# A ring of eight expert units instead of six, expert sums added straight into the residual, and a gather with the third tile's parts stacked on 128 rows

## What is computed

```python
def moe(x, router_w, router_b, w1, b1, w2, b2):
    logits = (x @ router_w).astype(jnp.float32) + router_b
    top_v, top_i = lax.top_k(logits, TOP_K)          # 4 of 32 experts
    gates = jax.nn.softmax(top_v, axis=-1)
    ...
    def expert_block(args):
        xblk, e = args
        hdn = xblk @ w1[e] + b1[e]                   # 1024 -> 2 x 1024
        g, up = hdn[:, :D_FF], hdn[:, D_FF:]
        g = jnp.minimum(g, SWIGLU_LIMIT)
        up = jnp.clip(up, -SWIGLU_LIMIT, SWIGLU_LIMIT)
        act = (up + 1.0) * (g * jax.nn.sigmoid(g * SWIGLU_ALPHA))
        return act @ w2[e] + b2[e]                   # 1024 -> 1024
...
    h2 = rmsnorm(x, ln_ffn_g) * (1.0 + sc2) + sh2
    f = moe(h2.reshape(B * L, D), ...)
    x = x + g2 * f
```

## Time and profile before

| | us |
|---|---|
| median of 3 runs | 1584.41 (1583.7 to 1587.89) |
| profiled execution | 1582.1 |
| its span, first to last instruction | 1580.3 |
| PE busy | 1483.1 (94%) |
| DVE busy | 527.3 (33%) |
| ACT busy | 336.7 (21%) |
| DMA, mean over the span | 313 GB/s, 495.14 MB |
| dense part and router | 0 to 594 |
| expert loop, 34 blocks | 594 to 1561 |
| mean granted TensorE clock | 0.974 of full |

### The profile page before, as it was taken

How to read it: one execution, slowest core, us unless ns; L and a number is a source line. 1 busy time by engine, 2 the same in 40 slices (tenths; PEclk the granted TensorE clock), 3 DMA queues, 4 the chain that set the end, 5 groups by cost and what they waited for, 6 DMA issues and landing times.

```text
span 1580.3 us, 20912 instructions
## 1 busy us (share of the span) xinstructions
PE 1483.1 (94%) x8280; PEld 626.6 (40%) x8281; DVE 527.3 (33%) x899; ACT 336.7 (21%) x607; POOL 131.2 (8%) x119
## 2 busy tenths in 40 slices
PE   4989899999999969999999999999999999999995
PEld 3456455554555443333333333333333333333331
DVE  2132124545257352332323323323333232332225
ACT  2123332212223232121211211211212121121110
POOL 0000001113238503000000000000000000000000
PEclk9989999999999969999999999999999999999997
DMA  9653533242324948999999999998877999999993
GB/s 345 236 233 134 237 135 132 89 143 88 120 94 148 315 176 336 429 429 428 429 428 428 429 428 429 428 429 365 335 302 290 430 427 430 427 429 428 428 430 136
DMA packets 40264, 495.14 MB, mean 313 GB/s; under 512 B 5316, under 2 KB 5860, under 8 KB 11428
## 3 DMA queue, kind: packets, MB, share of 16 engines
q1 hardware_dynamic: 35700, 480.18, 73.4%
q0 software_dynamic: 4528, 14.46, 3.3%
HBM read 490.14 MB, written 4.47 MB: 313 GB/s over the span
## 4 chain that ended last, share of the span: by engine, by line
PE 66%; DMA 27%; DVE 3%; ACT 2%; issue 1%; POOL 1%; SPq 0%; DVEq 0%
DMA ring<-in_w_moe 24%; PE ps L1759 20%; PE ps L1382 17%; PE ps L1785 9%; PE ps L1393 4%; PE ps L1713 3%; PE ps L1698 3%; PE ps L1335 3%; DMA ring<-in_w_dense 1%; PE ps L1351 1%; DMA T<-mod_rows 1%; DMA consts<-in_consts 1%; PE ps L1447 1%; PE ps L1766 1%; PE ps L1474 1%
## 5 line engine op out<-in xcount | busy, mean ns | idle before, releaser
L1759 PE MATMUL ps<-ring,arena 128*64 128x512 f32 x2176 | 485.5, 596 | 17.0 <-DMA ring<-in_w_moe 16.8
L1382 PE MATMUL ps<-ring,xT 128*128 128x512 f32 x672 | 302.7, 607 | 5.8 <-DMA ring<-in_w_dense 5.7
L1759 PEld LDWEIGHTS ps<-ring,arena 128*64 128x64 f32 x2176 | 150.9, 137 | 313.2 <-issue 271.0
L1785 PE MATMUL ps<-ring,arena 128*64 128x512 f32 x1088 | 248.5, 598 | 0.0
L1306 DVE SCALAR_TENSOR_TENSOR U<-ps,arena,U 128x1024 f32<-128x1024 f32 (+1 forms) x102 | 130.5, 1280 | 180.5 <-PE ps L1713 180.5
L1382 PEld LDWEIGHTS ps<-ring,xT 128*128 128x128 f32 x672 | 127.3, 193 | 159.8 <-issue 152.5
L1785 PEld LDWEIGHTS ps<-ring,arena 128*64 128x64 f32 x1088 | 72.1, 136 | 145.4 <-issue 130.9
L1297 DVE TENSOR_SCALAR arena<-ps 128x512 f32<-128x512 f32 x34 | 23.5, 692 | 241.5 <-PE ps L1766 241.5
L816 ACT ACTIVATE xT<-ps 128x512 f32<-128x512 f32 x35 | 20.9, 598 | 332.9 <-PE ps L1698 318.9
L1713 PE MATMUL ps<-xT,arena 64*128 64x512 bf16 x630 | 87.2, 384 | 2.9 <-DVE xT L1312 2.9
L1393 PE MATMUL ps<-ring,xT 128*64 128x256 f32 x672 | 78.6, 388 | 0.0
(11 more groups left out here) (298 smaller groups left out, 1166.6 us busy)
## 6 DMA issues: line engine op xcount, KB each, us to landing
ring<-in_w_moe SPq DMA_DIRECT2D x192, 2048.0 KB, 20.2
ring<-in_w_dense SPq DMA_DIRECT2D x33, 2048.0 KB, 8.5
V<-in_state POOLq DMA_DIRECT2D x6, 256.0 KB, 7.2
out_sample_retention<-V POOLq DMA_DIRECT2D x6, 256.0 KB, 4.9
arena<-in_b POOLq DMA_DIRECT2D x9, 128.0 KB, 2.8
R<-in_x_prompt SPq DMA_DIRECT2D x1, 1024.0 KB, 10.6
arena<-in_cache_kT POOLq DMA_DIRECT2D x8, 128.0 KB, 3.6
arena<-in_cache_v POOLq DMA_DIRECT2D x8, 128.0 KB, 4.0
```

The source lines that it names most:

```text
L1382: last = mm(banks[t][0], xT[:, k, t * P:t * P + P], wv[:, k, :], start=(k == 0), stop=(k == KD - 1))
L1759: last = mm(ps[64 * a:64 * a + 64, half, :], xgT[:, k, j % 2, :], wv[:, k, HALF * a:HALF * a + HALF], start=(j % 2 == 0 and k == 0), stop= ...
L1785: last = mm(ps[64 * a:64 * a + 64, 2, :], actT[:, k, j - 4, :], wv[:, k, HALF * a:HALF * a + HALF], start=False, stop=(j == 5 and k == 3), ...
```

## The change

**Ring.** `SLOTS` goes from 6 to 8: a unit may be loaded as soon as the one eight before it is used. The two new slots lie where `V`, `U` and `T` were: `memory` is one buffer of 8 x 4096 + 1024 columns, slot 6 covers V and the first row of U, slot 7 the other rows of U and two rows of T. Units 0 and 1 of expert 1 are loaded into them before the loop, the first after `x1_ready`, the second after `h_split`. Since 24 units (four experts) fill eight slots three times, the loops of SP and PE are written out for four experts: PE's block body stands four times, in a loop over groups of four, each with an inner loop over the blocks of its expert.

**Sums.** `U` is no longer an accumulator. Each scatter is multiplied by gate and gate2 rows into `grown` and added to R at once. The gate2 rows lie in dead parts of `mod` and in T's last row block; DVE waits for them (`gate2_in`) before its loop, no longer behind it.

**Gather.** ACT writes the middle part of tile 2 a second time to rows 64 to 127 beside its high part (`packed`), and doubles the tile's slot numbers (`slots_doubled`); one matmul on 128 rows then takes both.

```diff
-SLOTS = 6
+SLOTS = 8
+SPARE_SLOTS = 3
...
-    ring = sb("ring", [P, SLOTS, 4096])
+    memory = sb("memory", [P, SLOTS * 4096 + D])
+    ring = memory[:, 0:SLOTS * 4096].rearrange("p (s c) -> p s c", s=SLOTS)
+
+    def in_late_slots(n):
+        at = (DENSE_SLOTS + SPARE_SLOTS) * 4096 + 3 * D * n
+        return memory[:, at:at + 3 * D].rearrange("p (t d) -> p t d", t=3)
+
+    V, U, T = in_late_slots(0), in_late_slots(1), in_late_slots(2)
...
-    h_low = [V[:, 1, 0:HALF], V[:, 1, HALF:D], after_router[:, 1792:1792 + HALF]]
+    gate2 = [after_mod[:, 0:D], after_mod[:, 0:D], T[:, 2, :]]
+    h_low = [after_mod[:, D:D + HALF], low_1[:, :], W[:, 2, HALF:D]]
     h_parts = [[W[:, t, 0:HALF].bitcast(BF16), W[:, t, HALF:D].bitcast(BF16), h_low[t].bitcast(BF16)] for t in range(3)]
+    packed = W[:, 2, 0:HALF].bitcast(BF16)
...
@@ SP
         load_expert_unit(2)
+        load_rows(gate2[0], 10, gate2_in)
+
+        def load_second_expert(j):
+
+            sp.dma_start(ring[:, EXPERT_UNITS + j, :], ins["w_moe"][1, j, :, :]).then_inc(unit_in[EXPERT_UNITS + j], 16)
+
         sp.wait_ge(x1_ready, 3)
-        load_rows(V[:, 0, :], 10, gate2_in)
-        load_rows(V[0:64, 2, :], 10, gate2_in)
+        load_second_expert(0)
+        sp.wait_ge(h_split, 3)
+        load_second_expert(1)
+        load_rows(gate2[2][0:64], 10, gate2_in)
         sp.wait_ge(table_ready, 1)
...
+        with sp.Fori(0, NEXP // 4 - 1) as g:
+            for u in range(4 * EXPERT_UNITS):
+                if u % EXPERT_UNITS == 0:
+                    blocks = blocks_before(4 * g + (u // EXPERT_UNITS + 1))
+                e, j = divmod(u + SLOTS, EXPERT_UNITS)
+                sp.wait_ge(unit_used, EXPERT_UNITS * blocks + u % EXPERT_UNITS)
+                sp.dma_start(ring[:, u % SLOTS, :], ins["w_moe"][bass.ds(4 * g + e, 1), j, :, :].rearrange("a p n -> p (a n)")).then_inc(unit_in[u % SLOTS], 16)
...
@@ POOL
-        nc.gpsimd.memset(U[:, :, :], 0.0).then_inc(sum_clean, 1)
@@ ACT
+            if t == 2:
+                A(packed[64:128], T[0:64, t, :], ACT.Copy).then_inc(mid_moved, 1)
...
+        act.wait_ge(slots_placed, 1)
+        A(slot_of[64:128, 2, :], slot_of[0:64, 2, :], ACT.Copy).then_inc(slots_doubled, 1)
@@ DVE
-        dve.wait_ge(sum_clean, 1)
+        dve.wait_ge(slots_doubled, 1)
         dve.wait_ge(table_ready, 1)
         n_blocks = dve.value_load(table_i[0:1, MAX_BLOCKS:MAX_BLOCKS + 1], min_val=NEXP, max_val=MAX_BLOCKS - 1)
+        dve.wait_ge(gate2_in, 16 * (1 + BATCH_S))
...
             for t, r in enumerate(ROWS):
                 dve.wait_ge(scattered, 3 * i + t - 2)
-                both = U[0:r, t, :].rearrange("p (a b) -> p a b", a=2)
-                X.scalar_tensor_tensor(out=both, in0=ps[0:r, 6:8, :], scalar=gate_last[0:r, t:t + 1], in1=both, op0=ALU.mult, op1=ALU.add).then_inc(added, 1)
-            dve.wait_ge(added, 3 * i + 1)
+                X.scalar_tensor_tensor(out=halves(grown[0:r]), in0=ps[0:r, 6:8, :], scalar=gate_last[0:r, t:t + 1], in1=halves(gate2[t][0:r]),
+                                       op0=ALU.mult, op1=ALU.mult).then_inc(added, 1)
+                dve.wait_ge(added, 3 * i + t - 1)
+                X.tensor_tensor(R[0:r, t, :], R[0:r, t, :], grown[0:r], ALU.add).then_inc(summed, 1)
+                dve.wait_ge(summed, 3 * i + t - 2)
...
-        dve.wait_ge(gate2_in, 16 * (1 + BATCH_S))
-        for t, r in enumerate(ROWS):
-            X.tensor_tensor(U[0:r, t, :], U[0:r, t, :], V[0:r, 2 if t == 2 else 0, :], ALU.mult).then_inc(scaled, 1)
-            dve.wait_ge(scaled, t + 1)
-            X.tensor_tensor(R[0:r, t, :], R[0:r, t, :], U[0:r, t, :], ALU.add).then_inc(summed, 1)
-            dve.wait_ge(summed, t + 1)
...
@@ PE
             for t, r in enumerate(ROWS):
-                for m, part in enumerate(h_parts[t]):
+                parts = [(part, r) for part in h_parts[t]] if t < 2 else [(packed, P), (h_parts[t][2], r)]
+                for m, (part, rows) in enumerate(parts):
...
-        with pe.Fori(1, n_blocks + 1) as i:
-            e = pe.value_load(table_i[0:1, bass.ds(i - 1, 1)], min_val=0, max_val=NEXP - 1)
+
+        def expert_block(i, g, c):
+
+            def unit(j):
+                u = EXPERT_UNITS * c + j
+                pe.wait_ge(unit_in[u % SLOTS], 48 * g + 16 * (filled(u % SLOTS) + u // SLOTS + 1))
+                return ring[:, u % SLOTS, :].rearrange("p (k c) -> p k c", k=4)
...
+        with pe.Fori(0, NEXP // 4) as g:
+            for c in range(4):
+                before = pe.value_load(table_i[0:1, bass.ds(4 * g + (MAX_BLOCKS + 1 + c), 1)], min_val=0, max_val=MAX_BLOCKS - 1)
+                through = pe.value_load(table_i[0:1, bass.ds(4 * g + (MAX_BLOCKS + 2 + c), 1)], min_val=1, max_val=MAX_BLOCKS - 1)
+                with pe.Fori(before + 1, through + 1) as i:
+                    expert_block(i, g, c)
```

More of the change, by code:

```diff
@@ L1245, in _ @@
             aux_taken(dve, name)
-            done(X.tensor_scalar(s, s, 1.0, None, ALU.subtract))
+            done(X.tensor_scalar(s, s, 1.0, None, ALU.subtract), slots_placed if t == 2 else dve_step)
         done(X.tensor_copy(sel_now[:, 0, :], slot_of[:, :, 0]))
@@ L1323, in _ @@
             first = FINAL_BANKS[t]
[L1324 to L1327 removed]
+            X.scalar_tensor_tensor(out=halves(grown[0:r]), in0=ps[0:r, first:first + 2, :], scalar=gate_last[0:r, t:t + 1], in1=halves(gate2[t][0:r]),
+                                   op0=ALU.mult, op1=ALU.mult).then_inc(grown_last, 1)
+            dve.wait_ge(grown_last, t + 1)
+            X.tensor_tensor(R[0:r, t, :], R[0:r, t, :], grown[0:r], ALU.add).then_inc(final_ready, 1)
+            dve.wait_ge(final_ready, t + 1)
     @block.tensor
@@ L1695, in gather @@
             for t, r in enumerate(ROWS):
-                for m, part in enumerate(h_parts[t]):
+                parts = [(part, r) for part in h_parts[t]] if t < 2 else [(packed, P), (h_parts[t][2], r)]
+                for m, (part, rows) in enumerate(parts):
                     for a in range(2):
-                        last = mm(ps[64 * a:64 * a + 64, 3, :], pick[0:r, t, 0, :], part[0:r, HALF * a:HALF * a + HALF],
-                                  start=(t == 0 and m == 0), stop=(t == 2 and m == 2), skip_group_check=True)
+                        last = mm(ps[64 * a:64 * a + 64, 3, :], pick[0:rows, t, 0, :], part[0:rows, HALF * a:HALF * a + HALF],
+                                  start=(t == 0 and m == 0), stop=(t == 2 and m == 1), skip_group_check=True)
             last.then_inc(gathered, 1)
@@ L1754, in _ @@
                 for j in (2 * half, 2 * half + 1):
-                    pe.wait_ge(unit_in[j], 16 * e + 16 * (filled(j) + 1))
-                    wv = ring[:, j, :].rearrange("p (k c) -> p k c", k=4)
+                    wv = unit(j)
                     for k in range(4):
@@ L1773, in _ @@
             pe.wait_ge(act_ready, i)
-            for c in range(4):
-                last = tr(ps[:, 4, c * P:(c + 1) * P], h_act[:, c * P:(c + 1) * P], P)
+            for k in range(4):
+                last = tr(ps[:, 4, k * P:(k + 1) * P], h_act[:, k * P:(k + 1) * P], P)
             last.then_inc(actT_done, 1)
```

49 lines of the change are left out of this document (27 added, 22 removed).

## The result

The changed kernel takes 1573.43 us (median, 1569.57 to 1576.89) where the kernel before, on the same chip, takes 1587.72 (1583.7 to 1592.17): ratio 0.9906, 95% interval 0.9885 to 0.9927, faster by 14.3 us. The forecast, 1567.3 from 1584.4, is a ratio of 0.9892 and a gain of 17.1. The profiled execution took 1569.57 us, its span is 1567.8; against 1580.3 before that is 12.5 us less.

A forecast was written before the change was run, and what follows sets the result against it. PE and DMA were both taken as near their limit in the expert loop. Gains of 10.7 (block 18 to 34), 0.2 (block 34's gather) and 6.2 (tail) sum to 17.1 us: 1584.4 to 1567.3 us, range 1563.5 to 1577.5.

The forecast's parts named there:

- What bounds the kernel, and the sum of stages: PE and DMA both near their limit in the expert loop; gains 10.7 + 0.2 + 6.2 = 17.1 us.
- The ring in the gaps: Two DMA gaps at experts with two blocks: two more slots give 9.79 us of lead, once, not twice.
- Rival (b): The weight stream restarts no further on, the ring doing nothing: gain 7.3 us, 1577.1 us; chance 0.05.
- The start of the stream: Before the loop: unit 7's lead 1.7 us, net shift of the weight stream 0, from -1.7 to +4.3 us.
- Rival (c): The weight stream starts up to 4.3 us late for the row copies, all passed to block 18: 1571.6; chance 0.05.
- DVE's wait: DVE's first loop copy, now behind gate2_in, moves 7 us later, leaving PE 6.3 us late; price nothing.
- The gather: Third tile, 6 matmuls become 4: saves 0.215 us per block, 3.4 us from block 18 to block 34.
- Rival (a): The gather saves nothing, the change of row count eating it: gain 13.6 us, 1570.8 us; chance 0.09.
- Sums and tail: DVE's extra adds in the loop all hidden; the tail after the last block 6.2 us shorter.
- PE's loop at cost 0: PE's extra table read per expert and outer branch per four stay hidden, its sequencer being 2.4 us ahead: cost 0.
- (d): PE's fourfold loop needs one small code transfer at each return, 1.6 us beyond what is hidden: 1572.1; chance 0.08.
- (e): PE's code pages come one after another behind the weight stream, 10.8 us not hidden per return: slower, 1630; chance 0.05.

The follow-up runs named there:

- ring of six: The changed kernel with six slots instead of eight, the old loop start and nothing loaded ahead for the second expert: 1581.53 us, ratio 0.9972.
- late stream: The changed kernel with its last eight row copies made three times, each set waited for, ahead of unit 7: 1578.57 us, ratio 0.996.
- rows first: The changed kernel with the last eight row copies of gate2 ahead of unit 7 instead of behind it: 1570.55 us, ratio 0.9916.

## Why the prediction was right, step by step

- **What bounds the kernel, and the sum of stages.** Confirmed. By the stages counted from M, unrounded, the change gives -0.7 + 10.2 + 6.5 = 16.0 us; forecast were 0 + 10.7 + 0.2 + 6.2 = 17.1. The profiled spans differ by 12.5 only since this execution's M lies 3.5 later. Of the 6.1 us between 1573.4 and 1567.3, 3.3 is the kernel before, itself at 1587.7 in the comparison, 1.1 is the stages, and the rest is spread.
- **The ring in the gaps.** Right in mechanism and size: once, 9.8 us of the first gap used, the second unchanged, 9.6 us by the ring of six. The stage from block 18 to 34 gained 10.2 us instead of 10.7; 0.3 of the difference is a wait of 0.07 us in four of its blocks (below). The forecast had PE and weights arrive within 0.1 us of each other; the trace shows only that PE came last. Rival (b) is out.
- **The start of the stream.** Net shift 0 was forecast, +0.7 measured. Counted from M, unit 7 goes out at 27.4 where the forecast had 28.0 (603.3 - 575.3), and the rows behind it cost 1.3 instead of 2.0. The forecast's lead of 1.7 us was too large by 0.9, a mis-sized term: it took the slow start of unit 6 for time lost by the old stream alone (139 GB/s in the 2 us behind the issue, before), but unit 7 starts as slowly (131 GB/s in 606.27 to 608.27, after). Counted from issue to issue, the lead is one unit less the later issue, 4.9 - (28.0 - 23.9) = 0.8 us. An earlier issue and cheaper rows made up for it. With the measured times the shift is 27.4 - 23.9 - 4.9 + 1.3 = -0.1. The other 0.8 lies between the issue and block 18, and so does the 0.8 that was left over in the ring of six, which has the old start; I haven't found its cause. Rival (c) held in direction with 0.7 of its 4.3 us, and the late stream shows that any delay there arrives in full.
- **DVE's wait.** DVE's first copy 37.4 us after M (forecast 38.7), block 1 5.3 us longer than before (forecast 6.3), and nothing of it left at block 18; rows first takes the wait away and gains nothing.
- **The gather.** 27.67 to 27.46, 0.21 a block, as priced. Rival (a) is out.
- **Sums and tail.** 5.8 to 6.5 us in the tail (6.4 forecast with block 34's own gather), nothing in the loop.
- **PE's loop at cost 0.** Right for every return: blocks 4, 8, 26 and 30, which end in one, take 27.46 us. The 0.07 us more of blocks 3, 7, 20, 25, 29 and 33 belong to the third of the four bodies, not to the return: in block 33 they lie just ahead of the fifth unit, and the ring of six, with the same loop, has no such block. Wrong for the entry, where the sequencer isn't ahead: 1.0 us, and 1.2 of slow matmuls behind it. The change hides this behind units 6 and 7, the ring of six paid it. The lead of 2.4 us was read from block 5 and used for block 1.
- **Rivals (d) and (e).** Neither happened, but (e) is a real mechanism with a threshold closer than the forecast thought: at 1,264 instructions a return is free, at 1,920 PE stands for about 5 us at each, and at 2,528, with up to 2.7 of slow clock behind it, a return costs 8, above the 4.3 us from which the change would have been a loss if all returns had paid.

## What to carry to other kernels

When the stage before a bandwidth-bound loop ends, every microsecond by which the first transfer of the stream is late is paid at the end: look for what the first slots wait for, and put that work on whatever engine is idle (here 7.5 us by the stages, nearly half of what the change gave). Count a loop's instructions before unrolling it on PE: between 1,280 and 1,920 its returns turn from free to a halt of 5 us each, and to 8 us with the slow clock behind it. And compare executions by stages counted from a common point, since a wandering stage elsewhere hides effects of this size in the total.

## What the hardware showed that I had not expected

PE with a loop of 1,920 instructions stands for 4.8 to 5.3 us at every return, beside a weight stream at 416 to 423 GB/s, and the run has 33 more instruction packets; with 1,280 there is neither. In the 5.7 us after a halt of 5.3 (2,528 instructions) the granted clock was 0.50, which adds half again to its price. The dense part ends between 575.3 and 586.3 us in executions that do the same work there.
